# A two-block transformer in one program: the opening in one block, a token-major end, and the norm of the recurrence's heads token-major

## The reference

```python
def rmsnorm(x, g):
    return x * lax.rsqrt(jnp.mean(x * x, axis=-1, keepdims=True) + 1e-6) * g
# block one: h = x
#   u = rmsnorm(h, g_mix); q, k, v of 8 dilated and 8 block heads = u @ w_in; attention with a bias by distance
#   h = h + norm(y) @ w_out;  h = h + cross attention to rmsnorm(mem);  h = h + conv_ffn(rmsnorm(h));  rmsnorm(h, g_final)
# block two, two layers, on that h (latent) and ctx_2 (context): projection, then three mixers side by side,
#   8 neighbourhood heads, 4 heads of a recurrence run in both directions, a convolution of length 31;
#   the recurrence's output y of each direction and head (64 wide) is normalised over its head:
#     (y - mean) * rsqrt(var + 64e-5) * gn_g + gn_b,  times a gate, summed over the directions, plus a bonus
#   out projection; then an FFN (layer 0) or 8 experts, 2 of which serve a token (layer 1)
# output = rmsnorm(latent, final_g), 256 x 1024
```

## Time and profile before

| | |
|---|---|
| median of 3 runs | 3601.2 us (3599.58 to 3604.52) |
| the profiled execution | 3604.86 us |
| its span in the trace | 3603.1 us |
| granted clock of TensorE, mean over the span | 0.948 |
| TensorE busy | 3285.3 us (91%) |
| VectorE busy | 1041.6 us (29%) |
| ScalarE busy | 462.0 us (13%) |

### The profile page before, as it was taken

One profiled execution on the slowest core, in us unless ns is written; L12 is line 12 of the kernel. 1 busy time (PEld: TensorE's weight loads), 2 busy tenths in 40 slices (PEclk: granted clock), 3 DMA queues, 4 the chain that ended last, 5 costly groups with the idle time before them and its releaser, 6 DMA issues. The chain is left out here.

```text
span 3603.1 us, 37049 instructions
## 1 busy us (share of the span) xinstructions
PE 3285.3 (91%) x15201; PEld 1877.7 (52%) x15201; DVE 1041.6 (29%) x2036; ACT 462.0 (13%) x947; POOL 181.7 (5%) x225
## 2 busy tenths in 40 slices
PE   4988999979898789999979886699999999999998
PEld 3665788834457434444444475444444444444444
DVE  2236477536544532210037345300000000000001
ACT  0120100023132110000023221200000100000000
POOL 1000000000003200000000142000000000000000
PEclk9999999989879899999999898799999999999998
DMA  5315366611300033312222200198989888888984
GB/s 167 118 39 203 133 234 210 210 63 61 81 1 3 1 105 118 128 48 75 76 74 87 56 3 2 62 326 276 294 274 297 270 274 295 275 296 273 296 272 147
DMA packets 293206, 560.50 MB, mean 156 GB/s; under 512 B 29447, under 2 KB 42403, under 8 KB 293073
## 3 DMA queue, kind: packets, MB, share of 16 engines
q1 hardware_dynamic: 271959, 500.47, 42.5%
q0 software_dynamic: 13792, 50.52, 3.9%
q10 hardware_dynamic: 7322, 7.62, 0.8%
HBM read 557.36 MB, written 1.23 MB: 155 GB/s over the span
## 5 line engine op out<-in xcount | busy, mean ns | idle before, releaser
L1148 PE MATMUL bank<-normed,weight_ring 128*128 128x256 f32 (+1 forms) x2240 | 680.1, 466 | 73.9 <-PEq L1864 43.3
L1148 PEld LDWEIGHTS bank<-normed,weight_ring 128*128 128x128 f32 x2240 | 434.8, 195 | 312.6 <-issue 273.4
L2313 PE MATMUL bank<-weight_ring,work 128*128 128x512 f32 x1024 | 449.4, 593 | 10.1 <-ACT work L2346 10.1
L2313 PE MATMUL bank<-work 128*128 128x512 f32 x768 | 337.5, 592 | 0.0
L2313 PEld LDWEIGHTS bank<-weight_ring,work 128*128 128x128 f32 x1024 | 192.0, 190 | 241.1 <-issue 241.1
L654 PE MATMUL bank<-normed,weight_ring 128*128 128x512 f32 (+1 forms) x704 | 282.5, 562 | 24.7 <-PEq L1258 24.7
L1148 PE MATMUL bank<-work,weight_ring 128*128 128x256 f32 (+1 forms) x896 | 283.5, 477 | 9.2 <-PEq L1124 9.2
L2367 DVE TENSOR_TENSOR work<-bank,work 128x512 f32<-128x512 f32 x56 | 38.7, 692 | 787.8 <-PE bank L2313 787.8
L215 DVE SCALAR_TENSOR_TENSOR work<-work,small 128x512 f32<-128x512 f32 x336 | 237.6, 749 | 15.0 <-DMA work<-in_mod_w 7.9
L2313 PEld LDWEIGHTS bank<-work 128*128 128x128 f32 x768 | 144.7, 190 | 176.0 <-issue 176.0
L1148 PEld LDWEIGHTS bank<-work,weight_ring 128*128 128x128 f32 x896 | 172.4, 193 | 116.6 <-issue 102.9
(11 more groups left out here) (303 smaller groups left out, 2749.0 us busy)
## 6 DMA issues: line engine op xcount, KB each, us to landing
weight_ring<-in_moe_w_gate SPq DMA_DIRECT2D x64, 1024.0 KB, 5.1
weight_ring<-in_moe_w_up SPq DMA_DIRECT2D x64, 1024.0 KB, 5.1
weight_ring<-in_moe_w_down SPq DMA_DIRECT2D x64, 1024.0 KB, 5.1
work<-in_mod_w POOLq DMA_DIRECT2D x48, 1024.0 KB, 6.8
work<-in_moe_w_gate SPq DMA_DIRECT2D x48, 1024.0 KB, 5.1
work<-in_moe_w_up SPq DMA_DIRECT2D x48, 1024.0 KB, 5.1
work<-in_moe_w_down SPq DMA_DIRECT2D x48, 1024.0 KB, 5.0
weight_ring<-in_w_in SPq DMA_DIRECT2D x36, 1024.0 KB, 5.2
```

Source lines behind the costliest of these rows:

```text
L1148: last = nc.tensor.matmul(banks(gi)[j][:, 0:a.shape[-1]], w[:, k, j * P:(j + 1) * P], a, start=k0 + k == 0, stop=k0 + k == total - 1)
L2313: last = nc.tensor.matmul(self.bank[b], xg[:, kk], w[:, k], start=kk == 0, stop=kk == DT - 1)
```

## The change

Three stages are written anew.

The five blocks of the opening become one, `opening`. x is loaded first, half on SP's queue and half on ACT's, behind the resident tables; the vectors come in 26 loads, since arrays of both layers are joined, and alternate between SP's and ACT's queues; the weights' tiles come behind SP's share of them. POOL's queue brings the bucket tables, the relative bias, the zeros, mem and ctx. x is normed token-major: ScalarE squares a row of 1024 and accumulates, two small chains give 1/rms a token, a diagonal matrix of it is made, and TensorE multiplies x by that diagonal in place of the identity, which turns and scales at once; VectorE multiplies by the gain of the feature while it copies out. TensorE's order is: x turned plain, g_mix turned, x turned scaled, the bias lines, the vectors, mem, ctx.

`rwkv_out` norms `ytok` in place, token-major: sums over 64 columns by VectorE, the mean subtracted, squares on ScalarE, sums, small chains of 16 columns a direction, one multiply, and only then the squares are turned; ScalarE applies gain and bias while it moves them out of PSUM. In layer 1 it does so for the latent tokens alone (`t0, nt = 2, 2`).

The end: the last `rmsnorm` is gone. `store` turns the residual as it is, ScalarE squares from PSUM with an accumulator, and VectorE multiplies by 1/rms of the token and the gain, which lies as a row on all partitions, loaded as `final_gain` with the router; the output goes in four parts of 256 KB. `transpose_in`, `load_vectors`, `bias_lines` and `conditioning` are gone. Some tiles of the arena are taken in another order, so that they lie elsewhere.

```diff
+def opening(self, specs, memT):
...
     with nc.Block() as block:
+        @block.scalar
+        def _(act):
+            act.dma_start(self.table[:, :], ins["tables"][:, 0:RESIDENT_COLS]).then_inc(consts.sem, 16)
+            act.dma_start(tok[:, 0, 1], ins["x"][0, P:2 * P, :]).then_inc(xin.sem, 16)
+            act.wait_ge(cleared.sem, cleared.at(1))
+            for src, a, n in places[1::2]:
+                act.dma_start(rows[a % P:a % P + n, a // P, :], src).then_inc(vin_odd.sem, 16)
+            act.wait_ge(xin.sem, xin.at(32))
+            for t in range(2):
+                nc.scalar.activation(dump[:, t], tok[:, 0, t], ACT.Square, accum_out=st[:, t:t + 1]).then_inc(squared.sem, 1)
+            act.wait_ge(chain.sem, chain.at(2))
+            nc.scalar.activation(st[:, 4:6], st[:, 4:6], ACT.Sqrt).then_inc(rooted.sem, 1)
...
+        @block.sync
+        def _(sync):
+            sync.dma_start(tok[:, 0, 0], ins["x"][0, 0:P, :]).then_inc(xin.sem, 16)
+            sync.dma_start(grow[0:DT, :], ins["g_mix"][0].rearrange("(r p) -> r p", p=P)).then_inc(gin.sem, 16)
+            sync.wait_ge(cleared.sem, cleared.at(1))
+            for src, a, n in places[0::2]:
+                sync.dma_start(rows[a % P:a % P + n, a // P, :], src).then_inc(vin.sem, 16)
+            self.load_weights(sync, 0)
+            sync.wait_ge(linem.sem, linem.at(2))
+            for i in range(2):
+                sync.dma_start(self.bias_dram.ap()[8 * i:8 * i + 8, :], lines[0:8, i]).then_inc(stored.sem, 16)
+            sync.wait_ge(stored.sem, stored.at(32))
+            sync.wait_ge(rstored.sem, rstored.at(16))
+        @block.gpsimd
+        def _(pool):
+            pool.dma_start(tabs.rearrange("p a b -> p (a b)"), self.table_src("bucket_dil", "bucket_moba")).then_inc(bin_.sem, 16)
+            pool.wait_ge(cleared.sem, cleared.at(3))
+            pool.dma_start(rb[0:N_BUCKETS, :], ins["rel_bias"].rearrange("h b -> b h"), allow_slow_non_contiguous=True).then_inc(bin_.sem, 16)
+            pool.dma_start(bass.AP(self.rpb_dram, 0, [[254, n_rpb // 2], [1, 254]]), zero[0:n_rpb // 2, :]).then_inc(zstored.sem, 16)
+            for i, name in ((1, "mem"), (2, "ctx_2")):
+                pool.dma_start(tok[:, i], ins[name][0].rearrange("(t p) d -> p t d", p=P)).then_inc(win.sem, 16)
+            pool.wait_ge(zstored.sem, zstored.at(16))
+            pool.dma_start(self.rpb_dram.ap()[:, 48:79], ins["na_rpb_2"].rearrange("l h r c -> (l h r) c")).then_inc(rstored.sem, 16)
+        @block.tensor
+        def _(pe):
...
+            pe.wait_ge(consts.sem, consts.at(16))
+            pe.wait_ge(xin.sem, xin.at(32))
+            for t in range(2):
+                for b in range(2):
+                    turn(self.bank[2 * t + b], tok[:, 0, t], b).then_inc(raw.sem, 1)
+            pe.wait_ge(rawm.sem, rawm.at(1))
+            pe.wait_ge(gin.sem, gin.at(16))
+            nc.tensor.transpose(self.bank[0][:, 0:DT], grow[0:DT, :], ident[0:DT, 0:DT]).then_inc(gturned.sem, 1)
+            for t in range(2):
+                pe.wait_ge(diagm.sem, diagm.at(t + 1))
+                for b in range(2):
+                    for k in range(4):
+                        c = slice((4 * b + k) * P, (4 * b + k + 1) * P)
+                        last = nc.tensor.matmul(self.bank[4 + 2 * t + b][:, k * P:(k + 1) * P], tok[:, 0, t, c], diag[:, t], start=True, stop=True)
+                    last.then_inc(normed.sem, 1)
+            pe.wait_ge(cleared.sem, cleared.at(3))
+            pe.wait_ge(bin_.sem, bin_.at(32))
+            for i in range(2):
+                pe.wait_ge(rawm.sem, rawm.at(i + 2))
+                nc.tensor.matmul(self.bank[1 + i][0:8, :], rb[0:N_BUCKETS + 1, 8 * i:8 * i + 8], tabs[0:N_BUCKETS + 1, i], start=True, stop=True).then_inc(made.sem, 1)
+            pe.wait_ge(vin.sem, vin.at(16 * len(places[0::2])))
+            pe.wait_ge(vin_odd.sem, vin_odd.at(16 * len(places[1::2])))
+            pe.wait_ge(rawm.sem, rawm.at(4))
+            for g in range(groups):
+                last = nc.tensor.transpose(self.bank[3][:, g * P:(g + 1) * P], rows[:, g, :], ident)
+            last.then_inc(vturned.sem, 1)
+            pe.wait_ge(win.sem, win.at(32))
+            for i in range(2):
+                for t in range(2):
+                    for b in range(2):
+                        q = 2 * t + b
+                        if i == 0 and q == 0:
+                            pe.wait_ge(gmoved.sem, gmoved.at(1))
+                            pe.wait_ge(vmoved.sem, vmoved.at(1))
+                            pe.wait_ge(linem.sem, linem.at(2))
+                        if i == 1:
+                            pe.wait_ge(gmoved.sem, gmoved.at(q + 2))
+                        last = turn(self.bank[4 * i + q], tok[:, 1 + i, t], b)
+                        last.then_inc(wturned.sem, 1)
         @block.vector
         def _(dve):
             nc.vector.memset(rows, 0.0).then_inc(cleared.sem, 1)
+            nc.vector.memset(rb[0:64, :], NEG).then_inc(cleared.sem, 1)
+            nc.vector.memset(zero, 0.0).then_inc(cleared.sem, 1)
+            dve.wait_ge(squared.sem, squared.at(2))
+            nc.vector.tensor_scalar(st[:, 2:4], st[:, 0:2], 1.0 / D, EPS, ALU.mult, ALU.add).then_inc(chain.sem, 1)
+            dve.wait_ge(chain.sem, chain.at(1))
+            nc.vector.reciprocal(st[:, 4:6], st[:, 2:4]).then_inc(chain.sem, 1)
+            for i in range(2):
+                dve.wait_ge(raw.sem, raw.at(i + 1))
+                t, b = i // 2, i % 2
+                nc.vector.tensor_copy(xT[:, 4 * b:4 * b + 4, SEQ + t * P:SEQ + (t + 1) * P],
+                                      self.bank[i].rearrange("p (k n) -> p k n", k=4)).then_inc(rawm.sem, 1)
+            dve.wait_ge(rooted.sem, rooted.at(1))
+            for t in range(2):
+                nc.vector.tensor_scalar(diag[:, t], ident, st[:, 4 + t:5 + t], None, ALU.mult).then_inc(diagm.sem, 1)
...
+            dve.wait_ge(gmoved.sem, gmoved.at(1))
+            for i in range(4):
+                dve.wait_ge(normed.sem, normed.at(i + 1))
+                t, b = i // 2, i % 2
+                nc.vector.tensor_tensor(hT[:, 4 * b:4 * b + 4, SEQ + t * P:SEQ + (t + 1) * P], self.bank[4 + i].rearrange("p (k n) -> p k n", k=4),
+                                        gmix[:, 4 * b:4 * b + 4].unsqueeze(2).to_broadcast([P, 4, P]), ALU.mult).then_inc(gmoved.sem, 1)
...
+    t0, nt = (2, 2) if layer else (0, 4)
+    tok = slice(t0 * P, T2)
+    n = 4 * nt
+    sq, sums = ar.take("sq", 2, nt * RW_WIDTH), ar.take("head_sums", 2, 3, n)
+    o = ar.take("o", 4, nt * P)
+    heads = lambda x: x.rearrange("p (g k) -> p g k", k=HD)
+    rows = [y[:, d, t0:4].rearrange("p t n -> p (t n)") for d in range(2)]
+    spread = lambda x: x.unsqueeze(2).to_broadcast([P, n, HD])
...
+            for d in range(2):
+                nc.vector.tensor_reduce(sums[:, d, 0], heads(rows[d]), AX_X, ALU.add).then_inc(mean.sem, 1)
+            for d in range(2):
+                dve.wait_ge(mean.sem, mean.at(2))
+                nc.vector.tensor_scalar(sums[:, d, 0], sums[:, d, 0], 1.0 / HD, None, ALU.mult).then_inc(mean.sem, 1)
+                dve.wait_ge(mean.sem, mean.at(3 + d))
+                nc.vector.tensor_tensor(heads(rows[d]), heads(rows[d]), spread(sums[:, d, 0]), ALU.subtract).then_inc(centred.sem, 1)
+            for d in range(2):
+                dve.wait_ge(squared.sem, squared.at(d + 1))
+                nc.vector.tensor_reduce(sums[:, d, 1], heads(sq[:, d]), AX_X, ALU.add).then_inc(var.sem, 1)
+                dve.wait_ge(var.sem, var.at(3 * d + 1))
+                nc.vector.tensor_scalar(sums[:, d, 1], sums[:, d, 1], 1.0 / HD, RW_GN_EPS, ALU.mult, ALU.add).then_inc(var.sem, 1)
+                dve.wait_ge(var.sem, var.at(3 * d + 2))
+                nc.vector.reciprocal(sums[:, d, 1], sums[:, d, 1]).then_inc(var.sem, 1)
+            for d in range(2):
+                dve.wait_ge(rooted.sem, rooted.at(d + 1))
+                nc.vector.tensor_tensor(heads(rows[d]), heads(rows[d]), spread(sums[:, d, 2]), ALU.mult).then_inc(normed.sem, 1)
+            out = self.hT[:, 4:6, tok]
+            for d in range(2):
+                dve.wait_ge(gained.sem, gained.at(2 * d + 2))
+                x = o[:, 2 * d:2 * d + 2]
+                nc.vector.tensor_tensor(x, x, gate[d][:, :, tok], ALU.mult).then_inc(summed.sem, 1)
+                dve.wait_ge(summed.sem, summed.at(2 * d + 1))
+                nc.vector.tensor_tensor(out, bonus[:, :, tok] if d == 0 else out, x, ALU.add).then_inc(summed.sem, 1)
+                dve.wait_ge(summed.sem, summed.at(2 * d + 2))
         @block.tensor
         def _(pe):
+            for d in range(2):
+                pe.wait_ge(normed.sem, normed.at(d + 1))
+                for f in range(2):
+                    for t in range(nt):
+                        last = nc.tensor.transpose(self.bank[2 * d + f][:, t * P:(t + 1) * P], y[:, d, t0 + t, f * P:(f + 1) * P], self.tab("ident"))
```

(78 more changed lines are left out.)

301 lines of the change are left out of this document (88 added, 213 removed).

## The result

The changed kernel took 3567.8 us (median of 4 runs, 3567.25 to 3574.72) beside 3602.86 us for the kernel before on the same chip (4 runs, 3599.58 to 3605.43): ratio 0.9908, 95% interval [0.989, 0.9925]. Forecast were 3516 us, range 3506 to 3527: 35 us came of the 85. The profiled execution took 3568.13 us with a span of 3566.3.

A forecast was written before the change was run, and what follows sets the result against it. TensorE was 91% busy over the span, but the changed stretches were taken to stand in full on the path. Savings 40.5 + 14.3 + 21.5 + 10.2 - 1.2 = 85.3 us gave 3516 us, range 3506 to 3527.

The forecast's parts named there:

- Opening: Start to the projection's first matmul: at 27.5 us against 66.0, 38.5 saved; 40.5 saved with the clock's 2.
- (a): Opening, loading of x: x landed at 8.3 us, beside the tables, bucket tables and mem.
- (b): Opening, norm of x: squares by 10.8 us, diagonals at 13.1, normalising matmuls by 15 to 16.6, gain multiplies about 17.4.
- (c): Opening, bias lines' matmuls and two copies: done at 19 to 21 us; vectors' transposes and copy at 19.6 to 22.
- (d): Opening, 32 transposes of mem and ctx, waiting for (c)'s copy and GpSimd's queue: last copy ends at 24.3 to 30 us.
- (e): Opening, transfers: last weight at 24 to 25 us; the bias lines' store, queued behind weights, lands at 26 to 27.
- rival A: Opening held by transfers of mem and ctx: projection starts at 34 us, 8.5 less saved, 3524 us; chance 0.17.
- (f): Clock at the first projection's start: 2 of about 3 us lost at the lower clock come back, bounds 0 and 3.
- Head norms: Layer 0: 17.9 us against 32.11, 14.3 saved; layer 1, latent half only: 10.6 against 32.12, 21.5 saved.
- rival C: Head norms: strided sums at twice the price and waits between engines, 9 us less saved, 3525 us; chance 0.06.
- End, gain, experts: End 11.5 us against 21.66, 10.2 saved; final gain's load adds 1.2 before the router's matmul; expert stage stays at 1176 us.
- rival D: Expert stage: new allocation slows the weight stream below TensorE's demand, under 259 GB/s, 3530 to 3620 us; chance 0.02.

The follow-up runs named there:

- open_only: The kernel before with the new opening alone: six executions at 3559.0 to 3566.6 us, four at 3611.3 to 3616.7; ratio 0.9924.
- delay1: The changed kernel with a wait of VectorE for the stores and a memset at the end of the opening: 3514.25 us, one execution.
- norm_end: The kernel before with the new head norm, final gain and end alone, old opening kept: 3561.0 us, ratio 0.9875.
- after_again: The changed kernel unaltered, six more executions: three at 3518.0 to 3521.2 us, three at 3566.3 to 3574.5; ratio 0.9848.
- gap_before: The kernel before with a block in which VectorE clears y between first projection and first attention, lengthening TensorE's idle stretch: 3652.57 us, ratio 1.0145.
- layer_burst: moved_wait with ten dummy products ahead of the fifth unit's scores in layer 0's attention: 3501.97 us, ratio 0.9726.
- moved_wait: The changed kernel with fill3's dummies and the layers' attention waiting for tables only at the first unit with a bias: 3512.77 us, ratio 0.9754.
- fill3: The changed kernel filled with three dummy products behind the first projection: 3517.9 us, ratio 0.9761; taken again, 3517.86 us.

## Why the prediction was wrong: the steps against the profile

**Opening: right.** 28.16 for 27.5. The timeline of the changed kernel:

```profile
6.92 3.65 PE L1535 MATMUL bank<-tables,work 128*128 128x128 f32 x16 [6.92 <-DMA work<-in_x]
...
7.55 1.28 ACT L1495 ACT_TABLE_LOAD   x1 [7.55 <-issue]
...
12.93 5.28 PE L1551 MATMUL bank<-work 128*128 128x128 f32 x32 [0.57 <-DVE work L1594]
...
18.25 0.69 DVE L1606 TENSOR_TENSOR normed<-bank,small 128x512 f32<-128x512 f32 x1 [0.20 <-PE bank L1551]
...
21.60 3.68 PE L1535 MATMUL bank<-tables,work 128*128 128x128 f32 x32 [0.99 <-DVE work L1612]
...
24.01 2.48 DVE L1622 COPY residual<-bank 128x512 f32<-128x512 f32 x4 [2.17 <-PE bank L1535]
```

(a) x was there at 6.92, not 8.3. (b) Squaring needed a table load of its own, 1.28 us that the step lacks; x's early arrival made up for it, and the first products with the diagonal started at 12.93, for 13.1. What put the gains' end at 18.94 for 17.4 is these products: the step took them as 16 like the transposes, 1.9 us warm and 3.65 cold, but they are 32 instructions and took 5.28 us at a clock of 1.00. The errors of (a) and (b) go against each other; that is luck. (c) 21.3, inside its bounds. (d) The transposes waited for VectorE's copy and not for mem and ctx; the last copy ended at 26.5, inside its bounds. (e) What ended the opening is the bias lines' store, in SP's waits:

```profile
SPq L1485 <- DMA bias_lines<-work: 6.2, 1, 6.2
```

So rival A, the transfers of mem and ctx, is out, and the store behind the weights is in. (f) The projection's start was at 2.4 GHz here (2.8 us saved for 2) and at 1.2 GHz in the high execution above (3 us lost), so this differs between executions as well.

**Head norms: right.** 18.00 for 17.9 and 11.20 for 10.6 us. The sums, for which the earlier trace rows had no row of this width, cost what was taken, and rival C falls with them:

```profile
L1894 DVE TENSOR_TENSOR work<-work 128x1024 f32<-128x1024 f32 x2 | 2.5, 1226 | 0.1
...
L1889 DVE TENSOR_REDUCE work<-work 128x16 f32<-128x1024 f32 x2 | 2.3, 1214 | 0.9 <-PEq L1842 0.9
...
L1933 ACT ACTIVATE work<-bank,work 128x512 f32<-128x512 f32 x4 | 3.1, 777 | 2.3 <-PE bank L1920 2.0
```

The Trainium skill's warning of tensor_reduce on a hot path (VectorE: DVE Perf Modes, rules for kernel authors) has no ground in these rows: 1214 ns beside 1226 for a tensor_tensor of as many elements. ScalarE's moves took 0.78 us for 0.68 in layer 0, and 0.55 to 0.57 for 0.45 in layer 1, which is part of its 0.6.

**End, gain, experts: right.** The last transposes start at 3555.09 and the span ends at 3566.3, 11.2 us for 11.5. The table load stands alone, with no drain behind it: its activation starts 0.02 us after its end.

```profile
3559.47 1.28 ACT L2425 ACT_TABLE_LOAD   x1
...
3560.77 0.29 ACT L2425 ACTIVATE work<-work 128x1 f32<-128x1 f32 x2
```

The router's matmul came 1.87 us later than before behind layer 1's head norm, for 1.2 (bounds 0.4 and 3). The stream kept 278 GB/s, so rival D is out.

**What failed** is a step that seemed too plain to have a price: "what is taken out of one moves everything behind it forward". It moves it forward in time, but it doesn't carry the clock along. The first attention got no term and no row: it stood at 2.4 GHz in the one profile of before, and I took that for a property of the kernel. It is a draw: the level differs from one execution to the next. The kernel before was low in 3 of 36 executions (3653.7 to 3656.9 us, clock 0.933 to 0.934), the kernels with the new opening and an unaltered idle stretch ahead of the attention (the changed kernel's ten, open_only's ten, delay1) in 11 of 21. At one level the sum holds to a few us, as open_only and norm_end showed: outside the first attention the table has 89.05 us, and without the 4.63 of layer 0's attention 84.4, for 85.3. In the job of after_again the high executions give (medians) 3598.6 less 3521.0, 77.6 us, the low ones 3655.27 less 3572.83, 82.4, and the two high profiles 3603.1 less 3516.2, 86.9 (forecast 85.3); the filled kernel's 3517.9 is the forecast's 3516. The missing term is the price of the lower level in the first attention: 52.25 us. Had the changed kernel's first four executions been high, as three of its later six were, the forecast would have come true with the same step missing.

**What stays open.** That the idle stretch takes part in the decision is shown by gap_before (4.18 us: 4 of 4 low; 1.65: both levels); the fill agrees (0.30 us: 0 of 24 low) but adds dense products as well. Why the fall is likelier behind the new opening is not: theory 2 is wrong as a rule, since 10 of the 21 stayed high, but 11 of 21 against 3 of 36 (4 of 40 with norm_end, which keeps the old opening) is hardly chance, and no profile of before at the low level was taken to compare. Nor is it shown what decides between some 55 and some 66 us at 1.2 GHz in layer 0's attention.

## What to carry to other kernels

A saving can be read only between executions at the same level of TensorE's clock: across the levels this change is worth 35 us, at one of them 78 to 87. Before pricing a change, list the stages that start behind an idle stretch and run thin dependent loops, and give each a term for the other level (here 50 us for 32 units). If a short hole at a block's edge stands ahead of such a loop, three dummy products in it kept 24 executions of 24 at the higher level, and a burst put inside the running loop lifted it where it was low, while one ahead of the loop's own holes did not. And where two executions differ by the same amount again and again, take several before believing either.

## What the runs showed of the hardware, unexpected

- The same loop of dependent products ran at either speed. The first attention's 32 units took some 118 us at 1.2 GHz (112.77 to about 231), 3.7 us each, and 52 us less at 2.4 GHz, 2.1 each; at the lower level TensorE was busy 80.00 of 80 us (125 to 205) and the clock stayed at 0.50. The Trainium skill (TensorE: Matmul & The Clock Gate, A second HAM failure mode: psum-queue depth-cycling) tells of a clock that swings between its levels when the engine idles briefly, again and again, between groups of products that cycle through PSUM banks. This loop cycles through banks too, but had hardly any idle time (in the high execution 56.82 of 57.00 us busy, 125 to 182), and it didn't swing.
- A burst inside the loop brought the higher level: in layer_burst 20 instructions of 128x512 in 10.72 us stood ahead of a clock of 1.00 from 947 on; before the burst, 924 to 937, it was 0.56, and in moved_wait, without the burst, 0.50 from 947 to 980.
- The dummy products of float32 128x512 are two instructions each: 0.46 us an instruction in fill3 (six in 2.74 us), 0.48 over the 60 of layer 1 (clock 0.89), 0.59 over the 12 of layer 0 (clock 0.76). The 30 products took 29.00 us, where 9.52 us of idle TensorE had stood in fill3.
